# Remainders of fourteen rounded heads moved from VectorE to GpSimd in the last recurrence group

## The reference, cut to what matters

```
q, i_in, f_fw, f_bw, z = split(h @ w_in, 5)          # each 2048 wide: 16 heads of 128
k_d = (1 - lb_d) * sigmoid(-f_d);  log_f_d = log(lb_d + (1 - lb_d) * sigmoid(f_d))
S_t = diag(f_t) S_{t-1} + k_t v_t^T ;  o_t = S_t^T q_t   # forward and backward, summed
o = rmsnorm(o) per head * gain;   y = (o * silu(z)) @ w_out    # w_out is 2048 x 1024
x = x + gate * rmsnorm(y)
```

## Time and profile before

| | |
|---|---|
| median of 3 runs | 1785.49 us |
| profiled execution | 1785.29 us |
| its span in the trace | 1783.2 us |
| TensorE busy | 1719.9 us (96%) |
| VectorE busy | 1207.0 us (68%) |
| ScalarE busy | 901.2 us (51%) |
| GpSimd busy | 44.4 us (2%) |
| chain that ended last | PE 82%, DVE 6%, ACT 4%, DMA 3% |

### The profile page before, as it was taken

How to read it: one execution, slowest core, us unless ns; L and a number is a source line. 1 busy time by engine, 2 the same in 40 slices (tenths; PEclk the granted TensorE clock), 3 DMA queues, 4 the chain that set the end, 5 groups by cost and what they waited for, 6 DMA issues and landing times.

```text
span 1783.2 us, 35713 instructions
## 1 busy us (share of the span) xinstructions
PE 1719.9 (96%) x15070; PEld 1530.5 (86%) x15070; DVE 1207.0 (68%) x1673; ACT 901.2 (51%) x1096; POOL 44.4 (2%) x47
## 2 busy tenths in 40 slices
PE   6999999998999999999999999999999989999998
PEld 5877799987987789988888898898988967899896
DVE  5888755546678865545557768668677785577874
ACT  5564543335475443334645446455454553466772
POOL 2000000000000000000000000000000000000130
PEclk9999999998999999999999999999999999999999
DMA  8558568654457566655322222222212122352112
GB/s 197 189 189 299 150 169 198 189 190 147 147 180 270 204 165 185 184 193 179 86 85 72 73 72 73 74 71 84 72 61 84 61 96 95 113 169 69 49 60 106
DMA packets 254734, 238.28 MB, mean 134 GB/s; under 512 B 32288, under 2 KB 217680, under 8 KB 254320
## 3 DMA queue, kind: packets, MB, share of 16 engines
q1 hardware_dynamic: 253440, 233.21, 42.3%
q0 software_dynamic: 1136, 2.81, 0.6%
HBM read 234.94 MB, written 1.05 MB: 132 GB/s over the span
## 4 chain that ended last, share of the span: by engine, by line
PE 82%; DVE 6%; ACT 4%; DMA 3%; DVEq 2%; issue 1%; ACTq 1%; SPq 1%
PE pg L2540 35%; PE pg L1246 34%; PE pm L1246 7%; PE pm L2540 2%; PE pm L1249 2%; DMA ring<-in_ada_w 1%; DMA ring<-in_w_in 1%; DVE ring_r L567 1%; DMA ring<-in_hg_w_in 1%; PE pm L2543 1%; ACT ring_r L560 1%; DVEq L1734 1%; DVE ring L1732 1%; DVE ring_r L1698 0%; SPq L2163 0%
## 5 line engine op out<-in xcount | busy, mean ns | idle before, releaser
L567 DVE TENSOR_TENSOR ring_r<-ring,ring_r 128x2048 fp32r<-128x2048 f32 (+1 forms) x126 | 283.5, 2260 | 153.0 <-ACT ring_r L560 147.4
L1246 PE MATMUL pg<-ring_r,work_r 128*128 128x256 f32 (+3 forms) x1792 | 381.0, 324 | 4.5 <-DVE work_r L1704 3.4
L2540 PE MATMUL pg<-ring_r,work_r 128*128 128x512 f32 (+1 forms) x1776 | 379.3, 373 | 5.3 <-DVEq L3012 2.9
L2540 PEld LDWEIGHTS pg<-ring_r,work_r 128*128 128x128 f32 x1776 | 307.8, 190 | 68.6 <-issue 8.4
L1246 PE MATMUL pg<-ring_r 128*128 128x256 f32 (+3 forms) x1008 | 329.0, 326 | 2.5 <-DVEq L779 1.4
L1246 PEld LDWEIGHTS pg<-ring_r,work_r 128*128 128x128 f32 x1792 | 300.8, 190 | 29.9 <-DVEq L1699 3.4
L2540 PE MATMUL pg<-work_r,ring_r 128*128 128x256 f32 x2688 | 318.8, 281 | 5.9 <-DVEq L3002 3.1
L2540 PEld LDWEIGHTS pg<-work_r,ring_r 128*128 128x128 f32 x2688 | 317.4, 188 | 7.4 <-DVE ring_r L567 3.7
L560 ACT ACTIVATE ring_r<-ring 128x2048 fp32r<-128x2048 f32 (+1 forms) x126 | 237.2, 1890 | 167.8 <-DMA ring<-in_w_ffn_up 69.4
L1246 PE MATMUL pg<-work_r,ring_r 128*128 128x512 f32 (+1 forms) x976 | 263.9, 360 | 0.0
L1246 PEld LDWEIGHTS pg<-ring_r 128*128 128x128 f32 x1008 | 191.6, 190 | 17.6 <-DVEq L779 1.6
(11 more groups left out here) (380 smaller groups left out, 1854.9 us busy)
## 6 DMA issues: line engine op xcount, KB each, us to landing
ring<-in_hg_w_in SPq DMA_DIRECT2D x80, 512.0 KB, 4.0
ring<-in_w_in SPq DMA_DIRECT2D x36, 1024.0 KB, 5.1
ring<-in_ada_w SPq DMA_DIRECT2D x24, 1024.0 KB, 7.0
ring<-in_w_ffn_gate SPq DMA_DIRECT2D x44, 512.0 KB, 3.9
ring<-in_w_ffn_up SPq DMA_DIRECT2D x44, 512.0 KB, 5.3
ring<-in_w_ffn_down SPq DMA_DIRECT2D x22, 1024.0 KB, 4.8
ring<-in_w_out SPq DMA_DIRECT2D x12, 1024.0 KB, 4.9
ring<-in_ple_w_gate SPq DMA_DIRECT2D x8, 1024.0 KB, 4.8
```

Of the source, the lines that this page charges most:

```text
L567: W.low_done(V.tensor_tensor(lo, W.raw(i, name)[:, 0:lo.shape[1]], W.hi(i, name).bitcast(f32), ALU.subtract))
L1246: return T.matmul(out_, lhsT, rhs, start=first, stop=last)
L2540: return T.matmul(out_, lhsT, rhs, start=first, stop=last)
```

## The change

The fourteen subtractions of heads 0 to 13 are issued by GpSimd's queue, in order, each behind the ScalarE rounding of its head. They stand ahead of the wait on `h_free`. VectorE no longer issues them. It keeps heads 14 and 15, with a new wait ahead of them until all fourteen have been counted, and the weights' remainders.

```diff
@@ second_pool
             pool.dma_start(oT[:, 2048:2048 + INNER * BLOCK], d["hmask"]).then_inc(loaded_mask, 16)
+            for k in range(NH - GH):
+                pool.wait_ge(m_high, k + 1)
+                G.tensor_tensor(oT_lo[k], oT3[:, k, :], oT_hi[k].bitcast(f32), ALU.subtract).then_inc(m_low, 1)
             h_free.wait(pool, NG - 1)
@@ second_dve, group, the levels
                         for name in {2: ("hgo1",), 4: ("hgo2",)}.get(lev, ()):
                             piece_low(name)
-                        heads_low(*((2, 3), (3, 4), (4, 5), (5, 7), (7, 8), (8, 10), (10, 12))[lev])
@@ second_dve, group, after the levels
                     piece_low("hgo3")
-                    heads_low(12, 14)
@@ second_dve, group
                 if nxt and not after:
                     piece_low("hgo0")
-                    heads_low(0, 2)
@@ second_dve, after the groups
+            dve.wait_ge(m_low, NH - GH)
             heads_low(14, 16)
```

## The result

The changed kernel took 1789.59 us (median of 10 runs, 1786.61 to 1791.99) beside 1784.46 us for the kernel before (10 runs, 1782.10 to 1787.62). The ratio is 1.0028, 95% interval 1.0020 to 1.0037: 5.1 us slower. The forecast was 4.8 us slower, at 1790.3 us.

A forecast was written before the change was run, and what follows sets the result against it. VectorE was taken to bound only the last group's levels. GpSimd's 15.4 us, less 6.1 of VectorE work, 1.2 at the start and 3.1 beside keep and in gaps, gave 5.0 us on 1785.3: 1790.3 us, range 1780.5 to 1794.5.

The forecast's parts named there:

- VectorE bounds the stretch; removed work is a gain if nothing else happens: Last group's levels, 1430.98 to 1469.1 us: VectorE sets the pace, so removing its subtractions alone gains 4.4 us.
- my walk: Level-by-level timing of the last group without contention: keB at 1464.85 in place of 1469.16 us, 4.3 us earlier.
- Start's gain: Before the output step: two subtractions leave VectorE, so the first grow starts at 1429.76 in place of 1430.98 us.
- GpSimd is never late, its queue and the new wait cost nothing: GpSimd's fourteen subtractions, 18 us: heads ready before TensorE needs them, context transfer undelayed, the m_low wait met 20 us earlier.
- Contention at the upper bound: VectorE instructions with two SBUF inputs meeting GpSimd subtractions: each meeting costs 1.28 us, as at L2030; chance 0.48.
- Single turns, none between the products of a `grow`: Levels: GpSimd starts wherever VectorE has drained, never between a grow's two products; the walk ends 5.0 us late at keB.
- closer interleaving: Rival: GpSimd also takes turns between a grow's two products; about 8.1 us late, 1793.4 us; chance 0.15.
- The two walks: Last group timed without contention, 4.4 us gained, and with meetings at 1.28 us, 5.0 us lost; 9.4 us apart.
- The shift arrives at the end unchanged: After the levels, from 1469 us: TensorE sets the pace, so the 5.0 us delay at keB reaches the kernel's end.

The follow-up runs named there:

- e1_none: Changed kernel with the fourteen GpSimd subtractions left out, GpSimd only counting and TensorE reading rounded heads instead: 1780.34 us, ratio to before 0.9972.
- e3_two: Changed kernel, but only heads 0 and 1 are subtracted on GpSimd and VectorE keeps 2 to 13: 1783.84 us, ratio to before 1.0000.
- e9_three: e6_gated with head 7 back on VectorE, so GpSimd subtracts heads 0, 1 and 8: 1782.93 us, ratio to before 0.9992.
- e6_gated: e3_two with heads 7 and 8 also on GpSimd, started after grow of levels 4 and 5: 1781.92 us, ratio to before 0.9984.
- e8_aligned: Changed kernel, but GpSimd starts each pair from (2,3) to (12,13) only after a grow ends: 1785.94 us, ratio to before 1.0009.
- e5_copy: Changed kernel with GpSimd copying each unrounded head, one SBUF input, in place of subtracting: 1782.20 us, ratio to before 0.9992.
- e4_rest: Changed kernel, but heads 0 and 1 stay on VectorE and only 2 to 13 go to GpSimd: 1790.42 us, ratio to before 1.0041.

## Why the prediction was right, step by step

**VectorE bounds the stretch; removed work is a gain if nothing else happens**: right, by e1_none. The size was 3.4 us at the states, where my walk had 4.3 at keB. Its `grow` starts are 1.1, 1.2, 1.8, 1.9, 2.4 and 3.4 us early at levels 0, 1, 3, 4, 5, 6; I had 1.2, 1.5, 2.3, 2.6, 3.2, 4.3. (The sums used 4.4 for this gain, 0.1 more than the walk gives.) The hand-overs between the engines take a little more per level than I allowed.

**Start's gain, 1.22 us**: right, 1.12 us (first `grow` at 1431.39 - 1.53 = 1429.86 against 1430.98 us).

**GpSimd is never late, its queue and the new wait cost nothing**: right; the context transfer followed `h_free` as before, and no TensorE wait names L899.

**Contention at the upper bound**: right in kind. The price that I took from L2030 was 1.28 us; measured it is 1.10 us.

**Single turns, none between the products of a `grow`**: wrong. This was the rival "closer interleaving", and it is how the engines take turns. The second product of the level 0 pair, and the GpSimd instruction in front of it:

```profile
1432.53 2.32 DVE L1735 TENSOR_TENSOR ring<-ring,work 128x1024 f32<-128x1024 f32 x1
```
```profile
1432.20 1.57 POOL L899 TENSOR_TENSOR work_r<-work,work_r 128x512 fp32r<-128x512 f32 x1 [5.70 <-ACT work_r L963]
```

GpSimd's instruction starts at 1432.20 us, lasts 0.29 us longer than its 1.28 us because the first product is still running, and ends at 1433.77 us; the second product ends 1.08 us after that. The pair of 3.46 us is the sign that the prediction had named for this rival, "near 3.6 us". The rival's walk, at 1.28 us a meeting, ended 8.1 us late; measured are 6.4. The lower price of 1.10 us points that way; that it accounts for all of the difference is not shown.

The two walks lay 9.4 us apart (4.4 gained, 5.0 lost); the two kernels, e1_none and the changed one, lie 9.8 us apart at the states (3.4 gained, 6.4 lost). So the cost of the meetings was nearly met by two errors that point in opposite directions, turns too few and a price too high, and the gain was put 1 us too high. That the time came out at 1789.6 us for a forecast of 1790.3 us is in part luck, here and in the next step. By levels, in us late: forecast -1.2, +0.1, -0.3, +2.2, +1.9, +3.9, +5.0 and +5.0 at keB; measured -1.1, -0.1, -0.4, +0.5, +2.2, +4.8, +5.5 and +6.4.

**The shift arrives at the end unchanged**: nearly. 6.4 us at the states is 5.3 us at the end (6.8 us of span less 1.53). The missing 1 us is in the attention: from the first to the last GpSimd subtraction there the profiled execution of before takes 73.4 us (1661.07 to 1734.46), the changed one 72.4 us. The 1.26 us of L2030 in the earlier trace rows, a held instruction by itself, didn't occur in the changed kernel, where the longest of the sixteen is 0.62 us:

```profile
L2031 DVE TENSOR_SCALAR prm<-prm x16: 169/349/622, 1651.5 to 1734.2; 128x2 f32<-128x2 f32 x16
```

The other traces show which of the two is the odd one. In all eight experiments the longest of this instruction is 0.62 to 0.67 us, and the stretch takes 72.4 us in six of them and 72.7 to 72.8 in e3_two and e9_three. So it is the kernel before that lost 0.6 to 1 us there, in its one profiled execution. Measured against it, every other kernel stands better at the end than at the states, by 0.6 to 1.6 us (e6_gated 2.4 us early in place of 1.4, e8_aligned 1.2 late in place of 2.3). Whether the kernel before loses this in every execution, as it enters the attention in another phase, or did so by chance in that one, no run shows. The times can't tell it either: the interval of the change is 3.6 to 6.6 us.

## What to carry to other kernels

Moving an elementwise subtraction from a busy VectorE to an idle GpSimd isn't free even when nobody waits for the result: here a full meeting took 1.1 us from VectorE for 0.61 us given. Before such a move, look beside which VectorE instructions it will lie. Beside the work here that reads PSUM it was free; beside products, subtractions and copies from SBUF it wasn't. Gating all fourteen on the events that open PSUM windows cut the loss from 5.1 to 1.6 us. A gain came only with fewer of them: heads 0, 1 and 8 gave 1.5 us at the states, the other eleven stayed on VectorE. GpSimd instructions that only fill cost nothing here.

## What the runs showed of the hardware

In the levels' meetings the hold works both ways and by turns: whichever engine waits gets the next turn, even between two VectorE instructions that otherwise overlap by 0.08 us (two products of 1.22 us in 2.36 us). Not only two-input instructions of VectorE are held, but also fp32 copies from SBUF to SBUF on 32 partitions (0.89 to 1.47 us for three) and, in the attention, scalar operations on 128x2 elements (L2030, 0.17 to 1.26 us).

TensorE's granted clock fell behind some of the waits that the held VectorE caused. Windows of the changed kernel (columns: stretch, its length, busy time and count of PE, PEld, DVE, ACT and POOL, granted clock, DMA share, GB/s):

```profile
1466.00:1468.00 2.00, 0.00 (x0) 0.00 (x0) 2.00 (x2) 0.00 (x0) 0.53 (x1) 0.76 0.94 271
1468.00:1469.90 1.90, 0.00 (x0) 0.00 (x0) 1.64 (x4) 1.04 (x1) 0.00 (x0) 0.50 0.69 266
1469.90:1471.80 1.90, 1.87 (x65) 1.70 (x65) 1.85 (x3) 1.15 (x2) 1.13 (x1) 0.50 0.03 9
1471.80:1475.60 3.80, 3.80 (x16) 3.02 (x13) 3.40 (x3) 0.00 (x0) 1.37 (x2) 0.73 0.00 0
```

TensorE had stood idle for 5.0 us and was then granted 0.50, that is 1.2 GHz and not 2.4. The level's matmuls took 1.93 us (1.10 before) and the next head 3.98 us (about 3.0). Here the slow clock cost next to nothing, as the following `grow` ended only at 1475.39 us and the transposes began at 1475.61. In e8_aligned head 8, behind an idle of 3.5 us, took 4.61 us at a mean of 0.61, and the transposes followed at once:

```profile
1464.80:1469.20 4.40, 4.40 (x16) 3.42 (x13) 3.96 (x5) 0.12 (x1) 1.60 (x2) 0.61 0.01 4
```
```profile
1468.11 1.39 DVE L1760 COPY work<-pm 64x512 f32<-64x512 f32 x2 [0.23 <-issue]
```
```profile
1469.23 1.47 PE L1255 MATMUL pm<-cst,ring 128*128 128x128 f32 x12
1470.46 2.99 PE L1252 MATMUL pg<-ring_r,work_r 128*128 128x512 f32 x12
```

That is 1.6 us more than the 3.0 us of a head at full clock, but only about 0.3 us of it reached the states. The second half of those transposes, keB, also needs the copies of `keep`, which end at 1469.50 us; in the kernel before keB starts 0.06 us after them. It could so have started at 1469.56 us, and started at about 1469.83 (an estimate: the next head's 1470.46 less the 0.63 us that lie between the two before). The other 2.0 of the 2.3 us by which that kernel's states are late are there already at its last `grow`.

An idle's length alone doesn't decide. In the changed kernel the clock stayed at full behind 2.55 us of idle (first two rows), and so it did behind 2.0 us in e6_gated and 2.4 us in e5_copy. Behind 1.9 us it fell in e8_aligned, for heads 2 and 3 (third row), and in e4_rest, for head 1 (fourth row).

```profile
1452.10:1454.70 2.60, 0.06 (x1) 0.00 (x0) 2.15 (x3) 1.04 (x1) 0.35 (x1) 1.00 0.00 0
1454.70:1461.00 6.30, 6.29 (x88) 5.08 (x88) 5.05 (x4) 2.05 (x3) 3.52 (x2) 1.00 0.01 3
```
```profile
1438.53:1442.00 3.47, 3.47 (x13) 2.81 (x10) 3.02 (x4) 3.06 (x4) 0.72 (x1) 0.58 0.00 0
```
```profile
1434.14:1438.70 4.56, 4.56 (x22) 3.32 (x14) 3.82 (x4) 2.26 (x3) 0.00 (x0) 0.63 0.02 4
```

In e4_rest it was on the path. Head 1 took 4.62 us in place of 3.02, and level 2's matmuls began only behind it, 4.32 us after the start of level 1's `grow` where e1_none has 3.55: about 0.8 us of that kernel's 9.1 (an estimate from these two). What decides when the clock falls stays open.
